# Modulation of the second block as row products on VectorE beside the first block's feed-forwards, and block 2's first norms interleaved

## The reference, cut

```python
def conv_ffn(xn, w_up, conv_w, conv_b, w_down):                 # first block, each layer
    h = causal_depthwise_conv(xn @ w_up, conv_w) + conv_b
    g, u = jnp.split(h, 2, axis=-1)
    return (jax.nn.gelu(g) * u) @ w_down
...
def modulate(x, g, shift, scale):
    return rms_norm_2(x, g) * (1 + scale) + shift
...
def layer(x, xc, silu_c, silu_cc, lp, rope_mla, rope_gqa, update_ctx):   # second block
    mod = (silu_c @ lp["w_mod"] + lp["b_mod"])[:, None, :]      # w_mod is 1024 x 6144
    sh1, sc1, gt1, sh2, sc2, gt2 = jnp.split(mod, 6, axis=-1)
    modc = (silu_cc @ lp["w_mod"][:, :n_mod_c] + lp["b_mod"][:n_mod_c])[None, None, :]
    h = modulate(x, lp["g_norm1"], sh1, sc1)
    hc = modulate(xc, lp["g_norm1"], modc[..., :d], modc[..., d:2 * d])
    proj = h @ lp["w_in"]
...
    o_four = fourier_mix(proj[..., FOUR_START:GATE_START])
    x = x + gt1 * merge_branches(o_mla, o_gqa, o_four, proj[..., GATE_START:], lp)
    x = x + gt2 * conv_ffn_2(modulate(x, lp["g_norm2"], sh2, sc2), lp)
    if update_ctx: ...                                          # the same for xc, layer 0 only
```

## Time and profile before

| | |
|---|---|
| time, median of 3 runs | 2824.65 us (2824.44 to 2825.99) |
| the profiled execution's own time | 2824.05 us |
| its span | 2821.9 us |
| DVE busy | 628.7 us, 22% of the span |
| ACT busy | 531.0 us, 19% |
| POOL busy | 284.5 us, 10% |
| transfers | 331.7 MB, mean 118 GB/s |

### The profile page before, as it was taken

One profiled execution on the slowest core, in us unless ns is written; L12 is line 12 of the kernel. 1 busy time (PEld: TensorE's weight loads), 2 busy tenths in 40 slices (PEclk: granted clock), 3 DMA queues, 4 the chain that ended last, 5 costly groups with the idle time before them and its releaser, 6 DMA issues.

```text
span 2821.9 us, 29743 instructions
## 1 busy us (share of the span) xinstructions
PE 2727.7 (97%) x12102; PEld 1996.5 (71%) x12102; DVE 628.7 (22%) x1280; ACT 531.0 (19%) x1062; POOL 284.5 (10%) x280
## 2 busy tenths in 40 slices
PE   7999999999899999999999998999999999999999
PEld 5757877786677778845554445888864874887887
DVE  3023222111312221223530002111110225302220
ACT  1131122101212221102430001121200223202320
POOL 0010100000101000001330000000000003200110
PEclk9989999999999999999899999999999998999999
DMA  5322377533234765211002112112121130143342
GB/s 213 134 83 105 115 272 264 220 126 119 105 113 156 264 247 204 90 62 67 1 19 83 67 64 90 60 59 89 64 112 51 64 128 24 68 157 127 149 171 97
DMA packets 50815, 331.73 MB, mean 118 GB/s; under 512 B 2848, under 2 KB 31648, under 8 KB 31648
## 3 DMA queue, kind: packets, MB, share of 16 engines
q1 hardware_dynamic: 50720, 330.36, 31.5%
HBM read 329.30 MB, written 1.05 MB: 117 GB/s over the span
## 4 chain that ended last, share of the span: by engine, by line
PE 94%; DVE 3%; DMA 1%; POOL 1%; ACT 1%; issue 0%; DVEq 0%; SPq 0%; POOLq 0%; ACTq 0%
PE PS L643 27%; PE PS L548 25%; PE PS L2183 9%; PE PS L1139 5%; PE PS L1277 5%; PE PS L2187 4%; PE PS L963 3%; PE PS L1289 2%; PE PS L1780 2%; PE PS L608 2%; PE PS L974 2%; PE PS L986 1%; PE PS L428 1%; DMA arena<-in_mod 1%; PE PS L1896 1%; PE PS L2052 1%
## 5 line engine op out<-in xcount | busy, mean ns | idle before, releaser
L643 PE MATMUL PS<-XN,slot 128*128 128x256 f32 x3520 | 781.8, 384 | 15.8 <-DVE XN L488 10.9
L643 PEld LDWEIGHTS PS<-XN,slot 128*128 128x128 f32 x3520 | 672.0, 192 | 127.0 <-issue 18.1
L548 PE MATMUL PS<-arena,slot 128*128 128x256 f32 x1824 | 399.9, 381 | 10.1 <-POOL arena L1699 5.8
L548 PEld LDWEIGHTS PS<-arena,slot 128*128 128x128 f32 x1824 | 348.4, 191 | 61.1 <-POOL arena L1699 6.6
L548 PE MATMUL PS<-XN,slot 128*128 128x256 f32 (+1 forms) x1248 | 312.6, 411 | 5.0 <-DVE XN L488 5.0
L742 DVE SCALAR_TENSOR_TENSOR arena<-PS,small,arena 128x255 f32<-128x255 f32 (+2 forms) x352 | 168.8, 542 | 664.4 <-ACT arena L717 664.4
L548 PEld LDWEIGHTS PS<-XN,slot 128*128 128x128 f32 x1248 | 238.0, 191 | 76.7 <-issue 43.0
L2183 PE MATMUL PS<-XN,slot 128*128 128x512 f32 (+1 forms) x768 | 255.7, 486 | 1.0 <-ACT arena L1021 1.0
L2183 PEld LDWEIGHTS PS<-XN,slot 128*128 128x128 f32 x768 | 145.8, 190 | 102.9 <-issue 91.3
L717 ACT ACTIVATE arena<-PS,small 128x256 f32<-128x256 f32 (+1 forms) x176 | 99.2, 614 | 363.6 <-PE PS L643 363.3
L772 POOL TENSOR_TENSOR arena<-arena 128x256 f32 (+3 forms) x88 | 75.8, 862 | 821.5 <-ACT arena L720 821.5
(11 more groups left out here) (195 smaller groups left out, 2009.1 us busy)
## 6 DMA issues: line engine op xcount, KB each, us to landing
slot<-in_weights SPq DMA_DIRECT2D x86, 2048.0 KB, 7.8
arena<-in_mod SPq DMA_DIRECT2D x48, 1024.0 KB, 8.0
slot<-in_weights SPq DMA_DIRECT2D x16, 2816.0 KB, 9.4
slot<-in_weights SPq DMA_DIRECT2D x16, 2304.0 KB, 8.4
slot<-in_weights SPq DMA_DIRECT2D x2, 2176.0 KB, 8.8
slot<-in_weights SPq DMA_DIRECT2D x4, 1024.0 KB, 4.8
small<-in_small SPq DMA_DIRECT2D x1, 2693.0 KB, 19.2
SQ<-in_mem SPq DMA_DIRECT2D x1, 1024.0 KB, 5.7
```

What stands on the lines that cost most here:

```text
L548: mm = pe.matmul(o, l, r, start=k == 0, stop=k == len(terms) - 1, skip_group_check=True)
L643: mm = pe.matmul(o, slots[slot][:, a:a + P], XN[:, k, seg[g]], start=k == 0, stop=k == DK - 1, skip_group_check=True)
```

## The change

1. **Modulation on DVE.** tensor_mod_piece, add_modulation and DVE's copies of rows go. `w_mod` is laid out transposed, so that a piece holds 2 groups of 128 outputs (on the partitions) with all 1024 inputs along the row: again 24 pieces of 1 MB a layer, now in a ring of 3 buffers. silu(c) and silu(c_ctx) lie copied to all partitions (MODC, 1 MB, in_c). One output column is one `tensor_tensor_reduce` over 128x1024: product with MODC and its sum, 4 of them a piece. For c the product is written to PSUM banks 4 and 5, for c_ctx over the piece itself. Pieces stand after the convolution of the first three pairs of each turn (15), 3 after the up stage, 3 after the read of down job 0 and 3 after that of job 1. The transfer of a piece waits for DVE's last use of its buffer; in SP's queue the slabs of down jobs 2 and 3 stand behind three such transfers each. The load of MODC is issued after cross-attention; ACT applies silu to it (128x2048) at the start of the up stage.
2. **A semaphore of its own for convolutions** (`conv_done`). The PE's wait for an earlier pair's convolution counts on it, no longer on `vector_done`, in whose order the outputs of the norm ahead of the stage stand.
3. **add_out_halves:** ACT's squares and POOL's sums of x and context alternate for the first pieces, and DVE's norm of x stands one read earlier in `wo` of layer 0 (behind that of m=4, not of m=5).
4. **The last two steps of `four`** move from `heads` into `pairs` behind the scores of unit 1; in layer 1 the lead of the Fourier steps over the head tasks is 3 in place of 2. Two scratch buffers swap places (AB and SQ_GQ).
5. **The first gate** of `merge` (8 matmuls) moves into `pairs`, behind the scores' last unit; the waits for the attention's outputs move to just before the branch that reads them.

```diff
-        mod_slots = [area(16384, 8, T), H[:, 6:14, T:2 * T]]
-        SC = area(18432, DK, 32)
+        MODC = H[:, 0:DK, T:2 * T].rearrange("p (g j) t -> p g j t", g=2)
+        mod_slots = [area(13312 + 2048 * i, 2, 4, T) for i in range(MOD_RING)]
...
-        def tensor_mod_piece(pe, s, layer, p, turn):
...
-            for k in range(2):
-                for j in range(4):
-                    mm = pe.matmul(PS[32 * j:32 * j + 32, 4, 0:T], SC[:, 2 * i + k, :], w[:, k, j, :],
-                                   start=i == 0 and k == 0, stop=i == MOD_PARTS - 1 and k == 1,
-                                   skip_group_check=True)
...
+        def vector_mod_piece(dve, s, p, turn=None):
+            l = int(s[1])
+            i = p % MOD_RING
+            dve.wait_ge(sems[f"mod_landed{i}"],
+                        16 * ((MOD_PIECES * l + p) // MOD_RING + 1) + (16 * turn if turn is not None else 0))
+            for m in range(2):
+                for g in range(2):
+                    w = mod_slots[i][:, m, :, :]
+                    if g == 0 and (m or p not in (0, MOD_LOOP)):
+                        dve.wait_ge(*of(s, "mod_product", p if m else p - 1, 1 - m, turn=0 if turn is None else turn))
...
+                    op = dve.tensor_tensor_reduce(w if g else MODP, w, MODC[:, g, :, :], 1.0, 0.0, ALU.mult, ALU.add, total)
+                    if g == 0:
+                        op.then_inc(*tick(VD, s, "mod_product", p, m))
+            op.then_inc(*tick(VD, s, "mod", p))
...
                         elif half == 1:
-                            op.then_inc(*tick(VD, s, "conv", p))
+                            op.then_inc(*tick(CD, s, "conv", p))
...
+                if block == "a" and turn is not None and p < MOD_RING:
+                    if p == 0:
+                        dve.wait_ge(*of(s, "silu_c"))
+                    vector_mod_piece(dve, s, p, turn)
...
                     pair(p, turn, g % 2, (p % 2) * 2 * DK, 16 * (g // 2 + 1) + 16 * turn)
-                    if mod is not None:
-                        tensor_mod_piece(pe, s, mod, p, turn)
...
+            if block == "a":
+                act.wait_ge(sems["loaded_c"], 16 * (int(s[1]) + 1))
+                act.activation(MODC, MODC, ACT.Silu).then_inc(*tick(SD, s, "silu_c"))
...
-        def add_modulation(l):
...
-            lead = 4 if l == 0 else 2
+            lead = 4 if l == 0 else 3
...
-                    elif u <= len(fu):
+                    elif u < len(fu) - 1:
                         four(pe, u)
...
+                if u == 1 and early:
+                    early(pe)
...
+                if u == len(units) and late:
+                    late(pe)
...
+                    if u < 3:
+                        pe.wait_ge(*(of(f"batt{l}", "out", (n_out // 2 - 1, n_out - 1)[u]) if u < 2
+                                     else of(f"four{l}", "out", len(fu) - 1)))
...
-                            sp.wait_ge(*of(s, "mod", 2 * j + 1, turn=TURNS - 1))
-                            load_mod(base + 4 * TURNS - 1 + 2 * j, 1)
-                        for p in range(2):
-                            sp.wait_ge(*of(s, "mod", 4 * TURNS + p))
-                            load_mod(base + 4 * TURNS + 2 + p, p)
+                            for p in ((0, 1), (2,), (3, 4, 5), (6, 7, 8))[j]:
+                                sp.wait_ge(*(of(s, "mod", p, turn=TURNS - 1) if p < MOD_RING else
+                                             of(s, "mod", MOD_LOOP + p - MOD_RING)))
+                                load_mod(base + MOD_LOOP + p, p % MOD_RING)
```

More of the change, by code:

```diff
@@ L455, in shifts @@
-            def shifts(u):
-                for j, (o, _, _, shift, _) in enumerate(units[u]["outs"]):
-                    if shift is not None:
-                        act.wait_ge(*of(s, "scaled", u, j))
-                        act.activation(o, o, ACT.Identity, bias=shift).then_inc(*tick(SD, s, "out", u, j))
             for u in range(len(units) + 1):
                 if u < len(units):
-                    squares(u)
+                    if u >= units[u]["ring"]:
+                        act.wait_ge(*of(s, "rstd", u - units[u]["ring"]))
@@ L1236, in add_ffn, with add_out @@
                     then=(lambda pe: tensor_norm(pe, aside_s, aside_units)) if aside else None,
[L1237 to L1239 removed]
+                    needs=lambda k: (s, "h", k) if k >= PAIRS * TURNS else (s, "h", PAIRS - 1, "last"),
+                mod=s if block == "a" else None)
+        def add_out(s, rhs, ready, k_tiles, segs, gate=None, needs=None, then=None, mod=None):
             def reads(j, bank):
@@ L1261, in add_out, with vector @@
                 jobs[0]["needs"] = {i: [l for l in ls] for i, ls in jobs[0]["needs"].items()}
-            add_linear(s, jobs)
+            if mod is None:
+                add_linear(s, jobs)
+                return
+            def vector(dve):
+                for j, job in enumerate(jobs):
+                    reads_linear(dve, VD, "vector", s, [job], j)
+                    first = MOD_LOOP + MOD_RING * (j + 1)
+                    for p in range(first, min(first + MOD_RING, MOD_PIECES)):
+                        vector_mod_piece(dve, mod, p)
+                    if first == MOD_PIECES:
+                        vector_mod_end(dve, mod)
+            add(tensor=lambda pe: tensor_linear(pe, s, jobs), vector=vector)
         def add_out_halves(s, rhs, ready, k_tiles, last, gate, norms, x_at):
@@ L2093, in scalar_heads @@
                 stat(act)
-                for u in range(1, len(fu) + 1):
+                for u in range(1, len(fu) - 1):
                     four(act, u)
```

278 lines of the change are left out of this document (134 added, 144 removed).

## The result

The changed kernel takes 2731.19 us (median of 4 runs, 2727.12 to 2736.53) against 2824.55 (median of 4, 2823.19 to 2825.99) of the kernel before: a ratio of 0.9671, with a 95% interval of 0.9652 to 0.9689. That is 3.3% faster. The prediction was 2733.5 with a range of 2722 to 2757. The profiled execution took 2729.41 us, of which 2727.4 are its span, so 94.5 us less span than before.

A forecast was written before the change was run, and what follows sets the result against it. The PE, busy for 97% of the span, was taken as the bound. Gains of 68.5 + 2.6 - 1.5 + 14.3 + 6 + 1 = 90.9 us off 2824.05 gave 2733.2, as a median 2733.8, stated as 2733.5 us (range 2722 to 2757).

The forecast's parts named there:

- The PE's side of the modulation: Up stages of a0 and a1: without modulation they take 152.3 and 154.3 us, like b1, a gain of 68.5 us.
- The transposes: In a0 and a1: 1.74 us come back in a0 and 0.9 in a1, a gain of 2.6 us.
- The cost of a product: Modulation on DVE: a 128x1024 product with its sum takes 1.31 us, with 1.9 as a bound, hidden beside the PE.
- The point where the cover breaks: Up and down stages: DVE stays hidden until 1.87 us a product; from there each 0.1 us costs 9.6 us a layer.
- The chain of DVE alone: Up and down stages of a layer: DVE needs 50 + 96t = 176 us (t per product), the PE 229.4.
- rivals A and B: Modulation products on DVE too slow: A at half rate, 2828 us, chance 0.09; B above 2.38 us each, 2865 us, chance 0.05.
- Rival A: Modulation on DVE: an accumulating product takes 2.4 us, losing 14 us a layer; total 2828 us, chance 0.09.
- POOL beside DVE: Up loop: POOL's products and DVE's may hold each other; a turn reaches at worst 25.6 us, under 27.6, costing nothing.
- The slab behind the pieces: Down stages: slab 3 queues on SP behind pieces that DVE must first use up; charged -1.5 us (0 to -10).
- `wo` into b0: From the end of `wo` to b0: x's norm and b0 start earlier, 12.1 us plus 2.2 for the clock, 14.3 together.
- `heads` and `pairs`: Moved Fourier steps and longer lead: layer 1 net +5 us, layer 0 +1, together 6 (1 to 11).
- The gate: In front of `merge`: the moved first gate fills the PE's wait for ACT's copies, a gain of 1 us.

The follow-up runs named there:

- e11_fours_back_l0: The changed kernel with layer 0's last two Fourier steps back in `heads`, layer 1 unaltered: 2725.76 us, ratio 0.9646 to the kernel before.

## Why the prediction was right, point by point

**The PE's side of the modulation** was sized by one comparison, a0 and a1 against b1. The lengths that it gave for after, 152.3 and 154.3, came out as 152.0 and 154.0, and the gain as 69.0 against 68.5. That the gain is so close is in part luck, since the second trace of the kernel before would have made it 74. The transposes came as said too (2.6 against 2.7). With the products left out nothing changes, and with the modulation alone the up stages have the same 152.0 and 154.0: shown.

**The cost of a product** was bounded between 1.31 and 1.9 us and taken as 1.31. The instruction takes 1.22, and with an accumulator read inside it they start 1.15 apart. Both bounds were above the truth, since I added two durations that overlap. This was harmless, and the two-input operation with an accumulator takes as long as a reduction with one input: 1.22 us for 1024 columns against 1.225. The Trainium skill's sentence on half throughput ("Vector Engine (DVE) Microarchitecture Reference", points that are easy to get wrong) is on the scalar-tensor-tensor shape; the trace lists this operation as `CUSTOM_DVE_ANT_1`, and it shows nothing of a halving. Whether an accumulating scalar-tensor-tensor is halved no run here shows.

**The point where the cover breaks** was wrong: 1.87 us by a sum over the whole layer. At 1.7 the kernel already lost 41 us. The chain of DVE alone left out that the loop binds turn by turn, that DVE idles 3.1 us a turn for ACT, and that SP's queue ties slabs to DVE's progress. For the forecast it decided nothing, since t was 1.15; for rivals A and B it did. Rival A's 2828 would have been 2850 or more. Its own sum also holds a slip: the four terms it names, 14.3 + 6 + 1 + 2.6, are 23.9 and not 24.9, and its formula gives 2.37 us a product where the chain goes on with 2.39.

**POOL beside DVE.** Costed at nothing, and so it is. The holds are there: in the loop the second product of each piece, which meets POOL's, takes 1.74 us in place of 1.22, and POOL's product 0.99 in place of 0.86.

**The slab behind the pieces** (-1.5, 0 to -10) was 0 in the changed kernel.

**`wo` into b0** was predicted step by step, 12.1 us and 2.2 for the clock; 12.2 and 3.2 came. The two runs that undo the count and the norm's place each confirm their step: 5.5 to 6.5 against 6.0, and 2.5 against 2.5 with 0.9 of clock on top. The interleaving alone brings 1.0.

**`heads` and `pairs`** was the term that was mis-sized: 6 us and 1 for the gate, against 4.5 together. By the traces of before and after, layer 0 brought 2.3 where 1 and half of the gate were predicted, and layer 1 2.2 where 5 and the other half were. In layer 1 `heads` got 4.6 us shorter and not 3.8 + 3.3 = 7.1, since 1.25 us of the wait are left and the clock falls all the same; and `pairs` got 2.4 us longer even with the gate's 1.2 taken off, so some 3.6 where 2 was charged: the two steps take 7.1 us there from start to start at the low clock. With the steps in `heads` the lead alone is worth 4.0 there.

In layer 0 the number held and the mechanism did not. The step was "two steps move into a stretch at a clock of 0.55: the clock rises earlier, +1". It took the low clock of the trace of before for given. With the modulation moved and the steps left in `heads`, `pairs` starts at full clock in all four such traces (96.4 to 98.1 us to merge's first branch), and with the steps moved it starts cold in all eight (105.1 to 106.2). So beside the other parts of the change the move costs 6.4 us in layer 0. That the steps' place decides this is shown by e11_fours_back_l0; by what mechanism is not.

The gate brought 2.9 us where 1 was predicted, which hides part of the loss. That the sum came out within 2.3 us of the median is luck in part: 2.5 us too much here stand against 1.5 charged for a slab that came in time and 1.0 too little for `wo`, and 3.2 us of clock elsewhere had not been predicted by anybody.

**Open:** why the kernel before starts `pairs` of layer 0 at a low clock (0.50 and 0.57 over its first 16 us in its two traces) while the run with only the modulation moved starts it at full clock, though in both all of block b ahead of `heads` takes 148.5 us and `heads` 38.5. Open too is why `heads` of layer 1, with the same code, takes 28.8 us in some runs and 31.8 to 32.4 in others. No run here tells.

## What to carry to other kernels

Work moved to an idle engine is free only while the *loop's turn* on that engine is shorter than the PE's, with everything that the engine waits for in a turn counted in (3.1 us for ACT here). That point is to be worked out by turn, and with it what each queue holds behind a wait for the slower engine, since slabs that stand behind such a wait were 69 of 90 us of waits. A semaphore that counts everything an engine does makes a consumer wait for work it doesn't need: 6 us for one line. When matmuls are moved, measure the clock of the stretch behind the place they left, with the other parts of the change in place: here a stretch that got 3.4 us shorter made the one behind it 9.8 us longer.

## What the runs showed of the hardware

- A product with a sum over 128x1024, both inputs in SBUF, takes 1.22 us (median of 192) whether it writes to PSUM or to SBUF, and the read of its accumulator (0.08 to 0.14 us) lies inside its end: such operations start 1.15 us apart.
- A DVE operation with two SBUF inputs and a POOL operation hold each other: up to 2.28 us for 1.22 beside POOL's sums of 128x512, 1.74 beside its product of 128x256, which itself takes 0.99 us in the mean in place of 0.86.
- The clock's low stretches often repeat with the same code: 106.23, 106.24 and 106.23 us for one stage in three traces whose absolute times differ by up to 120 us. They need not: an unedited stage took 28.8 us in four traces of the changed kernel and its variants and 31.8 to 32.4 in five.
- A thousandth of mean granted clock goes with some 2 us of this kernel's time (2727.1 us at 0.983, 2736.5 at 0.978).
- ACT reloads a table, 1.28 us each time, ahead of the first centre tap of every turn of the up loop and again ahead of the gelu behind it; in a loop that binds on DVE this is part of the turn.
